# Rings of four for gate and up weights, a tail in pieces, and two loads requested later in the merge

## The reference, cut to what matters

```python
    merged = jax.nn.sigmoid(gt_d) * y_d + jax.nn.sigmoid(gt_s) * y_s
    return x + merged @ w_out, rows
...
def hier_moe(x, g_ffn, w_group, w_router, w_gate, w_up, w_down):
    h = rmsnorm(x, g_ffn).reshape(b * t, d)
    ...
    def add_expert(acc, params):
        wg, wu, wd, c = params
        act = jax.nn.silu(h @ wg) * (h @ wu)
        return acc + (act @ wd) * c[:, None], None
```

## Time and profile before

| | |
|---|---|
| time, median of 3 runs | 1240.65 us (1235.28 to 1244.28) |
| profiled execution, its own time | 1240.17 us |
| its span in the profile | 1238.4 us |
| TensorE, matmul busy | 1055.0 us, 85% |
| VectorE, ScalarE, GpSimd busy | 453.2, 246.2, 263.4 us |
| mean granted TensorE clock | 0.96 |
| DMA traffic | 304.14 MB, mean 246 GB/s |

### The profile page before, as it was taken

The page is one execution under the profiler, slowest core; times in us unless marked ns, Lnnn a source line. Parts: engine busy times, 40 slices in busy tenths (PEclk is TensorE's granted clock), DMA queues, the critical chain, the costliest instruction groups (busy, mean ns, idle before and its releaser), DMA issues. The chain is left out here.

```text
span 1238.4 us, 16090 instructions
## 1 busy us (share of the span) xinstructions
PE 1055.0 (85%) x6013; PEld 541.2 (44%) x6013; DVE 453.2 (37%) x1233; ACT 246.2 (20%) x537; POOL 263.4 (21%) x242
## 2 busy tenths in 40 slices
PE   4999899978998999888899969998777777778784
PEld 2554443434444445422256545554444444444441
DVE  4345888787564665302234423211111111011110
ACT  2012111211344455402014311111111001111110
POOL 1011101121454444000200013222222122222111
PEclk9999898989999999898999979999999999999997
DMA  5140122015575435687547659999999999999991
GB/s 182 34 160 23 65 85 94 27 68 175 167 230 191 124 120 158 234 291 278 184 184 293 219 192 400 402 391 396 405 409 403 407 400 405 402 402 408 400 384 34
DMA packets 77121, 304.14 MB, mean 246 GB/s; under 512 B 22402, under 2 KB 22402, under 8 KB 64754
## 3 DMA queue, kind: packets, MB, share of 16 engines
q1 hardware_dynamic: 61618, 273.47, 57.6%
q0 software_dynamic: 9824, 16.98, 4.8%
q10 hardware_dynamic: 5600, 12.65, 2.8%
HBM read 290.03 MB, written 29.66 MB: 258 GB/s over the span
## 5 line engine op out<-in xcount | busy, mean ns | idle before, releaser
L393 PE MATMUL p_z<-k_w,k_xT 128*128 128x512 f32 (+2 forms) x528 | 214.7, 562 | 8.1 <-DVE p_t L568 7.5
L393 PEld LDWEIGHTS p_z<-k_w,k_xT 128*128 128x128 f32 (+1 forms) x528 | 94.5, 193 | 115.2 <-issue 113.5
L816 PE MATMUL a_G<-k_w,k_xT 128*128 128x512 f32 x256 | 126.0, 616 | 2.5 <-ACT k_x L878 2.5
L1967 DVE TENSOR_TENSOR e_den<-e_sig,e_G 128x256 f32<-128x256 f32 x32 | 13.5, 421 | 273.6 <-ACT e_sig L1872 273.6
L1877 ACT ACTIVATE e_y<-e_Y,x_share 64x512 f32<-64x512 f32 x64 | 43.7, 683 | 316.7 <-PE e_Y L1780 299.3
L917 POOL TENSOR_TENSOR k_x<-k_x 128x512 f32<-128x512 f32 x64 | 80.5, 1270 | 99.3 <-DVE k_side L980 77.8
L1998 POOL DMA_INDIRECT out_y_p<-e_y,x_table x32 | 45.0, 1407 | 196.4 <-ACT e_y L1877 165.5
L151 POOL DMA_INDIRECT k_rows<-token_rows,x_table x32 | 31.3, 978 | 189.5 <-PE e_TX L1762 174.1
L816 PEld LDWEIGHTS a_G<-k_w,k_xT 128*128 128x128 f32 x256 | 44.0, 192 | 48.7 <-issue 44.3
L1171 PE MATMUL g_ring<-k_w,k_oT 128*128 128x512 f32 x128 | 61.9, 632 | 0.0
L1972 DVE TENSOR_TENSOR e_a<-e_den,e_U 128x256 f32<-128x256 f32 x32 | 13.5, 421 | 128.2 <-PE e_U L1768 128.2
(11 more groups left out here) (349 smaller groups left out, 1465.1 us busy)
## 6 DMA issues: line engine op xcount, KB each, us to landing
k_w<-in_w_in SPq DMA_DIRECT2D x11, 2048.0 KB, 7.9
k_w<-in_w_gate SPq DMA_DIRECT2D x11, 2048.0 KB, 44.9
k_w<-in_w_up SPq DMA_DIRECT2D x11, 2048.0 KB
k_xT<-in_w_down SPq DMA_DIRECT2D x11, 2048.0 KB
k_oT<-in_w_gate SPq DMA_DIRECT2D x11, 2048.0 KB
k_side<-in_w_up SPq DMA_DIRECT2D x11, 2048.0 KB
x_page<-in_w_down SPq DMA_DIRECT2D x11, 2048.0 KB
x_merged<-in_w_gate SPq DMA_DIRECT2D x10, 2048.0 KB
```

The source lines that it names most:

```text
L393: last = nc.tensor.matmul(z[u % 3][0:p, 0:WIDTH[k]], s.xT[:, j, 128 * i:128 * i + p], s.w[:, c % 2, j, 0:WIDTH[k]], start=j == 0, stop=j = ...
L816: last = nc.tensor.matmul(G[u % 2][:], s.xT[:, j, 128 * i:128 * i + 128], s.w[:, q % 2, j, :], start=j == 0, stop=j == KD - 1)
L1967: v.tensor_tensor(den[:], sig[:], G[j][:, 0:HW], ALU.mult).then_inc(chain, 1)
```

## The change

Five things change together.

1. Gate and up weights get rings of four places, down weights keep three. The fourth gate place is the first four tiles of s.x, the fourth up place consists of three parts: two unused rows of rowbuf, the last tile of s.x, and a new tile e_up. The load of expert 3's gate weights is requested at the end of the merge, behind the stores of rows; that of its up weights is the first in the next block. SP then follows a list, LATER: up to expert 7 the gate and up loads of an expert come before the down load of the one before it, from expert 8 on behind it. The tiles sig, den and a become one (hid), which makes room.
2. The last down load is split in four, one for each quarter of the product's sum, and the down product of expert 31 waits for each part by itself.
3. The extra blocks are worked out behind experts 28 to 30 and after 31, in the memory of a gate place (DVE first waits for the product that uses it last). Each engine can read their number as soon as it is there (extra_counted). POOL reads it before its last additions, and SP, at the end, waits for their landing.
4. POOL's gathers for experts 0 and 1 move from the merge's end to the start of the experts' block.
5. In the merge, w_out is requested when all 32 "vd" pages are multiplied (v_used 32 where it was 24), and the prompt rows when all 64 value pages are.

```diff
-DEPTH = 3
+DEPTH = (4, 4, 3)
+FIRST, SETTLED = 3, 8
...
-EXTRA_AT = 2
+EXTRA_AT = NE - 4
 EXPERT_WEIGHTS = ("w_gate", "w_up", "w_down")
 
 
+LATER = [(FIRST, 1)]
+for _e in range(FIRST + 1, NE):
+    LATER += [(_e, 0), (_e, 1), (_e - 1, 2)] if _e < SETTLED else [(_e - 1, 2), (_e, 0), (_e, 1)]
+LATER += [(NE - 1, 2)]
+
+
 def load_expert(eng, io, s, e, n):
 
-    eng.dma_start(s.ew[n][e % DEPTH], s.expert(io[EXPERT_WEIGHTS[n]], e, n)).then_inc(s.ew_in[n][e % DEPTH], 16)
+    r = e % DEPTH[n]
+    for b, part in s.ew[n][r]:
+        eng.dma_start(part, s.expert(io[EXPERT_WEIGHTS[n]], e, n)[:, b:b + part.shape[1], :]).then_inc(s.ew_in[n][r], 16)
+
+
+def weights_in(s, e, n):
+
+    return s.ew_in[n][e % DEPTH[n]], 16 * len(s.ew[n][e % DEPTH[n]]) * (e // DEPTH[n] + 1)
+
+
+def weight_row(s, n, r, b):
+
+    return next(part[:, b - first] for first, part in s.ew[n][r] if first <= b < first + part.shape[1])
...
             sp.wait_ge(summed, 2 * TILES)
             load_expert(sp, io, s, 2, 2)
+            sp.wait_ge(s.x_stored, 16 * TILES)
+            sp.wait_ge(s.h_stored, 16 * TILES)
+            load_expert(sp, io, s, FIRST, 0)
...
-            pool.wait_ge(v_used, 3 * NPAGE * NS // 4)
+            pool.wait_ge(v_used, NPAGE * NS)
             for h in range(2):
                 pool.dma_start(w_out[:, h], io["w_out"][0][:, W * h:W * h + W].rearrange("(j p) c -> p j c", p=128)).then_inc(w_out_in[h], 16)
-            pool.wait_ge(v_used, NPAGE * NS)
             nc.gpsimd.memset(aZ[:], 0.0).then_inc(zeros_ready, 1)
             pool.wait_ge(zeros_ready, 2)
             pool.wait_ge(orr_ready, 1)
             nc.gpsimd.tensor_tensor(orx[:], orr[:], mh[:], ALU.pow).then_inc(o_rs, 1)
+            pool.wait_ge(v_used, 2 * NPAGE * NS)
             pool.dma_start(s.x[:, 0:NT, :], io["x_prompt"][0].rearrange("(i p) d -> p i d", p=128)).then_inc(x_in, 16)
...
-            pool.wait_ge(s.h_stored, 16 * TILES)
-            pool.wait_ge(table_ready, 1)
-            for n in range(2):
-                gather_rows(nc, s, n, s.table[:, n:n + 1])
...
-        sig, den, a = sb("sig", [128, HW]), sb("den", [128, HW]), sb("a", [128, HW])
+        hid = sb("hid", [128, HW])
+        sig = den = a = hid
+        s.ew[1][FIRST].append((4, sb("up", [128, 4 * DE]).rearrange("p (j c) -> p j c", c=DE)))
...
-        def down_product(bank, r):
+        def down_product(bank, r, arrivals=()):
             for b in range(4):
+                if arrivals:
+                    nc.tensor.wait_ge(*arrivals[b])
                 for h in range(2):
                     last = nc.tensor.matmul(bank[CAP * h:CAP * h + CAP, :], aT[:, b % 2, CAP * (b // 2):CAP * (b // 2) + CAP],
-                                            s.ew[2][r][:, b, W * h:W * h + W], start=b == 0, stop=b == 3)
+                                            weight_row(s, 2, r, b)[:, W * h:W * h + W], start=b == 0, stop=b == 3)
             return last
 
-        def extra(eng, step):
-
-            eng.wait_ge(extra_ready, 1)
-            n = eng.value_load(s.ctl[0:1, NX:NX + 1], min_val=0, max_val=NX)
+        last_in = [sem(f"last_in{b}") for b in range(4)]
+        LAST_ARRIVALS = [(last_in[b], 16) for b in range(4)]
+
+        def last_in_pieces(sp):
+
+            for b in range(4):
+                sp.dma_start(s.ew[2][(NE - 1) % DEPTH[2]][0][1][:, b:b + 1, :], s.expert(io["w_down"], NE - 1, 2)[:, b:b + 1, :]).then_inc(last_in[b], 16)
...
+        def extra_blocks(eng):
+
+            eng.wait_ge(extra_counted, 1)
+            return eng.value_load(s.ctl[0:1, NX:NX + 1], min_val=0, max_val=NX)
+
+        def extra(eng, step, n=None):
+
+            n = extra_blocks(eng) if n is None else n
             with eng.If(n > 0):
+                eng.wait_ge(extra_ready, 1)
...
-            for e in range(DEPTH, NE):
-                for n, done in enumerate((g_done, u_done, d_done)):
-                    sp.wait_ge(done, e - DEPTH + 1)
+            for e, n in LATER:
+                if e >= DEPTH[n]:
+                    sp.wait_ge((g_done, u_done, d_done)[n], e - DEPTH[n] + 1)
+                if (e, n) == (NE - 1, 2):
+                    last_in_pieces(sp)
+                else:
                     load_expert(sp, io, s, e, n)
...
+            sp.wait_ge(y_added, 32 * NE)
...
+                arrivals = LAST_ARRIVALS if e == NE - 1 else ()
+                if not arrivals:
+                    pe.wait_ge(*weights_in(s, e, 2))
                 if e >= 2:
                     pe.wait_ge(y_out, e - 1)
-                down_product(Y[j], r).then_inc(d_done, 1)
+                down_product(Y[j], e % DEPTH[2], arrivals).then_inc(d_done, 1)
+            pe.wait_ge(extra_in, 1)
+            for m in range(M):
+                p = ROWS[m // 2]
+                last = nc.tensor.matmul(TB, Rk[0:p, m, :], Wk[0:p, m].rearrange("p x b -> p (x b)"), start=m == 0, stop=m == M - 1,
+                                        skip_group_check=True)
+            last.then_inc(extra_tabled, 1)
...
+                if e == EXTRA_AT:
+                    blocks_of_experts()
+                if e == EXTRA_AT + 1:
+                    slots_of_blocks()
+                if e == EXTRA_AT + 2:
+                    tables_of_blocks()
+            tables_out()
...
+            pool.wait_ge(s.h_stored, 16 * TILES)
+            for n in range(2):
+                gather_rows(nc, s, n, s.table[:, n:n + 1])
...
+                if e == NE:
+                    n_extra = extra_blocks(pool)
                 if e:
                     pool.wait_ge(y_out, e)
                 if e >= 2:
                     pool.wait_ge(y_added, 32 * (e - 1))
                 if e:
                     add_rows((e - 1) % 2, s.table[:, e - 1:e], s.to_s[:, e - 1:e])
-            pool.wait_ge(y_added, 32 * NE)
...
-        s.ew = [[s.w[:, 0], up(s.oTs[:].rearrange("p k j t -> p (k j t)")[:, 0:KD * DE]), up(flat(s.merged[:]))],
-                [s.w[:, 1], up(s.side[:]), s.w_out[:, 0]],
-                [down(flat(s.xT[:])[:, 0:4 * D]), down(flat(s.page[:])), down(flat(s.w_out[:, 1]))]]
-        s.ew_in = [[sem(f"ew_in{n}{j}") for j in range(DEPTH)] for n in range(3)]
+        whole = lambda *slots: [[(0, ap)] for ap in slots]
+        x, spare_rows = s.x[:].rearrange("p t d -> p (t d)"), s.rowbuf[:, 0:2].rearrange("p n w -> p (n w)")
+        s.ew = [whole(s.w[:, 0], up(s.oTs[:].rearrange("p k j t -> p (k j t)")[:, 0:KD * DE]), up(flat(s.merged[:])), up(x[:, 0:KD * DE])),
+                whole(s.w[:, 1], up(s.side[:]), s.w_out[:, 0]) + [[(0, up(spare_rows)), (2, up(x[:, KD * DE:]))]],
+                whole(down(flat(s.xT[:])[:, 0:4 * D]), down(flat(s.page[:])), down(flat(s.w_out[:, 1])))]
+        s.ew_in = [[sem(f"ew_in{n}{j}") for j in range(DEPTH[n])] for n in range(3)]
```

49 lines of the change are left out of this document (17 added, 32 removed).

## The result

The changed kernel takes 1221.64 us (median of 4 runs, 1220.91 to 1222.75), the kernel before 1240.74 on the same chip. The ratio is 0.985, with a 95% interval from 0.981 to 0.989. On a second chip it was 0.987 (0.982 to 0.991; experiment 4). That is 19.1 us faster. The forecast was 28.2 faster, at 1212.0, with a range from 1202 to 1226, and 1203 to 1219 as the likeliest case's own range.

A forecast was written before the change was run, and what follows sets the result against it. The prediction took the experts' stream of 2 MB weight loads, 5.58 us each, plus a tail to set the end. Its terms 11 + 6 + 8 + 0.8 + 2.4 = 28.2 us off 1240.2 gave 1212.0, range 1202 to 1226.

The forecast's parts named there:

- likeliest case: Whole kernel: the forecast of 1212.0 us holds, with 1203 to 1219 as its own range; chance 0.62.
- Part 1: Merge: requesting the output weight behind the "vd" pages ends their slow slot; net 11 us, bounds 3 and 15.
- given back: 3.2: Merge, next slot: two or three pages come at 2.1 us instead of 0.7 beside the output weight, costing 3.2 us.
- Rival A: Merge: the output weight only moves the page wait to the "vs" slots; Part 1 falls to 3, 1220 us; chance 0.15.
- Part 2: Merge: prompt rows requested behind all value pages, so the last eight pages run clean; 6 us, bounds 4 and 8.
- Part 3: Start of experts: rings of four put the weight stream two loads ahead (11.2 us), less a later start; net 8 us.
- Part 4: Tail: last down load in pieces gains 0.8 us; POOL's drain starting without its wait gains 2.4 us.
- the product's 5.35 us stay: Tail: the last down product itself keeps its length of 5.35 us, so no gain there.
- Part 5: Late experts and end: moved extra-block arithmetic and table products stay hidden under other work, costing nothing.
- Rival B: Start of experts: first gather late, DMA engines dry before expert 4's load; Part 3 gives 1 to 4, 1217 us; chance 0.12.
- Rival C: Start of experts: expert 3's load isn't brought forward, its stores landing last; Part 3 at 0, 1220 us; chance 0.05.
- Rival D: Expert loads: 19 more requests from the pieces pay fixed time in line, 3.2 us each, 1273 us; chance 0.04.

The follow-up runs named there:

- experiment 4: The changed kernel, unaltered, run again on a second chip: 1220.86 us, ratio 0.987.
- w_out_last: The changed kernel with the output weight requested behind the 64th value page, just ahead of the prompt rows: 1213.20 us, ratio 0.979.
- no_lead: The changed kernel with rings of four kept, but expert 3's loads and later ones requested only when the kernel before did: 1227.62 us, ratio 0.991.
- experiment 10: The changed kernel with every gate and up load requested in quarters, 176 more requests: 1229.99 us, ratio 0.993.
- merge_only: The kernel before with only the merge's two requests (output weight, prompt rows) moved as in the change: 1230.75 us, ratio 0.993.
- old_end: The changed kernel with the last down load whole and POOL waiting for its own last additions, as before: 1223.87 us, ratio 0.986.
- Experiment 8: w_out_last with expert 3's loads requested only when the first gather has landed: 1214.17 us, ratio 0.978.

## Why the prediction was right, and where its sizes were off

The direction and the stated range (1202 to 1226) held. The likeliest case did not hold as stated: 1221.64 lies outside its 1203 to 1219, and the range held because it had been made wide enough for rivals A and B, a part of each of which came. By the profiles 9.0 us are missing (28.2 less 19.2): 4.9 in the merge (17 less 12.1), 3.6 in the rings (8 less 4.4), 1.9 in the common code ahead, less 1.4 more at the end (4.6 where 3.2 was forecast). The last gain was luck, a faster clock in the last product that the prediction had put at nothing.

**Part 1 (output weight, 11 us)** is mis-sized, and through its give-back. The "vd" slot became clean as forecast: 17.0 us of creeping are gone, TensorE idles 0.55 us in 551.6 to 567. The step "given back: 3.2" failed. It let two or three pages of the next slot be late. In the profile a whole slot creeps: from the product ahead of it to its last page it takes 12.9 us where it took 6.4, with the clock at 0.93 over the stretch, and w_out_last got 7.7 us more by taking the weight away from there. The gate rows come late as well, but TensorE waits for none of them. Rival A, at 0.15, named this mechanism, though not its size (part 1 at 3); its argument of 26 us of bytes in some 26 us of time was the right one, and a DMA share of 0.65 over a stretch that is full in its first part was a poor answer to it. The trace agrees at the new place, too, with the rule cited there (the Trainium skill, DMA: Bandwidth & Descriptors, section Queues, rings and completion order: a DMA engine takes its queues in turn): a page beside the weight landed after 8.2 us, slowed and not stopped.

**Parts 1 and 2 together (17 us)** gave 12.1 by the profiles, and by times 8.7 alone and 3 to 6 beside the rest. The sum was made from one execution whose merge was slow, 129.9 where the same order of requests also took 120.3. Part 2 by itself held as far as one profile tells: the last slot runs without waits beyond 0.42 us, and from the product behind the second "vs" slot to the last value matmul it takes 16.6 us instead of 21.8, 5.2 less where 6 was forecast. Neither part was run alone, so their shares rest on the profiles.

**Part 3 (rings, 8 us)**: the mechanism is shown by no_lead: the two loads of lead are worth 5.6 us by the profiles and 5.5 to 7.6 by the times. The start delay was close: by the profiles of before and after 4.1 of the 11.2 us of lead are lost between expert 2's down load and expert 4's (in before, expert 3's) gate load, where 3.3 was forecast, and the gather took 7.3 where I took 8. What the sum left out is the stream's rate. Of the 7.1 us left there, 4.7 are still there at the last U product (4.4 in the means). In the first profile of each, 84 loads take 1197.37 - 727.04 = 470.3 us where 86 took 1211.14 - 732.00 = 479.1: 5.60 each against 5.57. So "still 5.6 us a load" held, and yet it cost 2.4 us over the whole stream. Which part of it the up loads in three pieces have stays open; at 0.05 us a request the 16 of them are 0.8 us. SP's long requests (experiment 10) came with the change as well; whether they cost the stream anything was not tested.

**Part 4 (pieces 0.8, drain 2.4)** measured 0.7 and 2.6. The step "the product's 5.35 us stay" was wrong: it is 3.65 in all eleven profiles of the changed kernel and its variants and 5.35 in the three of before and merge_only, worth 1.7 us. The granted clock is the difference (1.00 against 0.72). Neither the pieces nor a shorter wait ahead of the product makes it (old_end has neither: 1.21 us of wait, in before 1.23), nor the order of the loads, which no_lead has as before. Two things near the product are in all eleven and in none of the three, and were not tested apart: the last U product reads its weights from the three parts of the fourth place, and twenty small products for the tables follow right behind the down product (at 1206.40). Which of them it is, if it is one of them, is not shown.

**Part 5 (hidden)** held: nothing of the extra-block work stands on the chain that ended last, and from the start of the last U product to the end of the last Y it takes 9.1 us, 2.4 less than before.

**Rival B** (dry DMA engines) is real in small: 0.65 of DMA share in 718 to 732. Experiment 8 started expert 4's load sooner, and the time stayed the same. **Rival C** is out: expert 3's load goes at 709.02, ahead of the gather. **Rival D** is out by a factor of 60. The 2.0 us a request that it takes from the Trainium skill (DMA: Bandwidth & Descriptors, section Anatomy of one DMA) stand there for POOL's requests, while the 19 are SP's; paid in line they are out in the same way.

**The signs set down.** Two of the three that were to prove the prediction wrong came. A "vs" slot grew by more than 5 us (6.4 to 12.9). And the first gate product ends 5.0 us earlier (727.04 against 732.00), less than 10; counted from the first gate load, which takes the common code out, it is 9.6. The third, a load over 5.7 us, stayed away (5.60). Of the signs in favour, the slot of "vd" pages took 6.3 us and not under 6, the last value matmul came 9.0 us earlier (13.7 counted in the same way) and not 15 to 19, and the first wait for weights came at expert 11 where it was at 9, two experts later and not four or five. The clean last slot (0.42 us of waits) and the traffic up to the first gate product (257 GB/s from 704.03 on) came as said. The drain lasts 10.5 us, not 7.7, but it starts before the last scatter and ends 7.9 after it. So the time was in range, while the working of part 1 was not confirmed.

## What to carry to other kernels

When a large transfer is moved away from waits, follow it to where it lands: sum the bytes that everybody asks for between its request and its first use, and move it until it lies under work that asks for none, which was worth 7.7 us more here than the change got. Cost a stretch full of short waits from several profiles, because waits and clock made two executions of one kernel differ by 13.6 us. At the boundary of a stage fed by a stream of weights, protect the start of the stream, not the first product. Look at the signs you set down as well as at the time: here the time fell into the range and two signs said that a step of the working was wrong. The best version found is w_out_last: 0.979 of the kernel before.

## What the runs showed of the hardware

- One program's merge took 120.3 and 133.9 us in two executions, with granted clocks of 0.82 and 0.66 in the slot that waits for pages and 1.00 and 0.86 in a stretch that waits for nothing.
- The gather of an expert's rows by POOL took 3.05 us alone and 7.3 beside 4 MB of weights that SP had requested. Two loads of 1 MB took 5.4 and 15.7 us without and with 4 MB requested by POOL beside them.
- POOL's drain at a block's end ends 7.9 us after its last scatter when it follows at once (1211.8 to 1219.7). After a wait for the landing it still takes 7.7 to 7.9 by itself. With two gathers under way beside weights it took 8.7, and 4.4 without the weights.
- With 2 MB loads in four requests each, one more request costs 0.05 us of the kernel's time. SP's own time for a request of a whole load was 0.33 us in the median in the kernel before and up to 4.2 by tile in the changed one; for a quarter it was 0.9 to 1.6.
- The last down product took 5.35 us at a granted clock of 0.72 and 3.65 at 1.00, the same 16 matmuls.
